# The beginning of a two-block transformer kernel: order of the modulation columns, and who multiplies them

## The chip, the cores and the metric

The kernel runs on one core of a Trainium2 chip. The metric is the device time of one execution in microseconds (us). Of three runs of the kernel before, the median is 2067.61 us.

## The reference

Two transformer blocks in turn on x (256 rows, 1024 columns, float32). The first has two layers with modulation. What the change touches is how layer 0 begins:

```
c_act = silu(c)                                  # 1024 values
mod = c_act @ ada_w[layer] + ada_b[layer]        # 1024 x 6144, gives 6 x 1024 values
sh1, sc1, g1, sh2, sc2, g2 = split(mod, 6)
h = rms_norm(x, norm_mix[layer]) * (1.0 + sc1) + sh1
x = x + g1 * mixer(h, ...)                       # begins with proj = h @ w_in[layer]
```

The mixer (three kinds of attention), a dense feed-forward part, a second layer with eight experts, and a second block (a state-space branch, windowed attention, a feed-forward part) follow. They are the same in both kernels.

## The kernel before, in words

All weights come as one stream, in slots of up to 1 MB, by DMAs that the SP queue issues in the order of the program. Layer 0 begins before the ring of slots is in use. Eight early slots (`EARLY_SLOTS`) hold the 2048 columns of `ada_w[0]` that make shift and scale. A unit `u` is 512 columns, slots 2u and 2u+1; slot 2u holds the row blocks k = 0 to 3, slot 2u+1 the row blocks 4 to 7. A slice is one k of a unit: 128 rows by 512 columns. Behind the early slots come the first ring slots (`load_to(3)`), which hold the first columns of `w_in`.

`mod` is wanted as columns: 128 values of it down the partitions, block by block. Two engines share a unit's eight slices.

- VectorE (`dve_mods`) takes the first `SUMS[u]` slices: each is multiplied by its value of `cact` per partition and added into `modsum` (128 x 512). The sum over the partitions is missing, and TensorE makes it in `pe_mods_sum`: four products of 128 columns of `modsum` with a column of ones.
- TensorE (`pe_mods`) takes the rest straight from the slot: four products for each slice, with one column (`cact`) as the moving side. Both add into the same PSUM bank, 2 or 3 by turns (`COLUMN`).
- `dve_mods_add` adds the bias and writes four columns of `K.mod`.

Once scale and shift of the first four blocks of 128 columns are there, `turned_part(0, 4)` forms these blocks of h, turned (they were transposed by `pe_turn` into PSUM), as a high and a low part (`hT`, `hTl`). `turned_part(4, 8)` forms the other four. Weights are split in a high part (ScalarE, `whi`) and a low part (VectorE, `wlo`) in parts (chunks) of a slot; `split_to(n)` brings the splits up to chunk n, and `BETWEEN` says at which blocks j of the forming the splits of the first stage `inA0` come in between. Every large product is three matmuls: high by high, high by low, low by high. `inA0` has four chunks of 12 matmuls of 416 columns.

Each engine runs a program written out in order by hand: `pe_start`, `dve_start`, `act_start`, then the mixer. An instruction waits for the semaphore counts of named events (`wait_ge`). In `pe_start` stand idle matmuls, `idle(n)`: n products of 128 x 128 by 256 columns of `colt` into bank 1, whose result nobody reads. The root of the row norms (`dve_eps`, `dve_root`) gives the factors that `pe_along` lays along the free dimension; `turned_part` waits for them.

Order before on TensorE: 10 idle, block of unit 0, 2 idle, closing sum 0, 1 idle, transposes of x, 3 idle, unit 1, 2 idle, sum 1, factors, 4 idle, unit 2, 2 idle, sum 2, 8 idle, unit 3, 2 idle, sum 3, 2 idle, projection.

Of the kernel before, what the change touches and what calls it, by code (L numbers as in the profile page):

```python
# [10 lines left out]
ALU = mybir.AluOpType  # L11
# [65 lines left out]
def ada(layer, c0, c1):  # L77
    return panels(f"ada{layer}", "ada_w", (layer,), KT, c0, c1)
# [7 lines left out]
def plan():  # L86
    p = []
    for l in range(2):
        into = [panels(f"inA{l}", "w_in", (l,), KT, 768, 1184), panels(f"inD{l}", "w_in", (l,), KT, 0, 512),
                panels(f"qup{l}", "w_q_up", (l,), 2, 0, 768) + panels(f"kvup{l}", "w_kv_up", (l,), 1, 0, 1024),  # L90
                panels(f"inB{l}", "w_in", (l,), KT, 1184, 1696),
                narrow(f"inV{l}", "w_in", (l,), 512, 768) + narrow(f"inV{l}", "w_in", (l,), 1696, 1952)]
        mod = summed(0, 2048) if l == 0 else []
        behind = {(1, 0), (1, 1), (2, 3), (3, 0)}
        for n, stage in enumerate(into):
            for at, slot in enumerate(stage):
                p.append(slot)
                if mod and (n, at) in behind:
                    p.append(mod.pop(0))
        if l == 0:  # L100
            p += summed(0, 3072) + summed(0, 4096)
        p += tapered(f"out{l}", "w_out", (l,))
        if l == 0:
            ffn = gate_up("ffn", "ffn_w_gate", "ffn_w_up", (0,)) + down("ffnd", "ffn_w_down", (0,))
            mod = summed(0, 5120) + [slot for c in range(0, 6144, 1024) for slot in summed(1, c)]
            for n, slot in enumerate(ffn):
                p += [slot] + (mod[n - 2:n - 1] if n > 1 else [])
        else:
            for e in range(NE):
                p += gate_up(f"moe{e}", "moe_w_gate", "moe_w_up", (0, e))  # L110
                p += down(f"moe{e}d", "moe_w_down", (0, e))
    w = "w_in_2"
    xbc = blocks_t("xbc", w, (0,), list(range(XBC0, XBC0 + 4096, 128)))
    p += xbc[:5] + panels("dt", w, (0,), KT, DT0, DT0 + 32) + xbc[5:]
    for c in (Q0, K0, V0):
        p += narrow("qkv0", w, (0,), c, c + 512)
    p += panels("z", w, (0,), KT, Z0, Z0 + 2048)
    p += panels("gs", w, (0,), KT, GS0, GS0 + 1024)
    p += panels("sproj", "w_ssd_proj_2", (0,), 16, 0, D)
    for g in (1, 2):  # L120
        for c in (Q0, K0, V0):
            p += narrow(f"qkv{g}", w, (0,), c + 512 * g, c + 512 * g + 512)
    p += narrow("ga", w, (0,), GA0, GA0 + 1024)
    p += panels("aproj", "w_attn_proj_2", (0,), 4, 0, D)
    p += tapered("out2", "w_out_2", (0,))
    p += blocks_t("up2", "w_up_2", (0,), [c for b in range(FT) for c in (128 * b, FF + 128 * b)])
    p += down("down2", "w_down_2", (0,))
    return p


def whole_plan():

    return ada(0, 0, 2048) + plan()


def offsets(p):
# [7 lines left out]


EARLY_SLOTS = 8

COLS = {}

# [79 lines left out]
class Tensor(Unit):  # L229
# [23 lines left out]
    def idle(self, b, n):  # L253

        self.take(b)
        for _ in range(n):
            self.mm(self.K.ps[b][:, 0:256], self.K.cst("ones"), self.K.cstt[:, 0:256], True, True)
# [369 lines left out]
def pe_start(K, pe):  # L627

    def idle(n):
        for _ in range(n):  # L630
            pe.mm(K.ps[1][:, 0:256], K.colt[:, 0:128], K.colt[:, 0:256], True, True)
    pe.wait_ge(K.s_cols, 32)
    idle(10)
    pe_mods(K, pe, 0)
    idle(2)
    pe_mods_sum(K, pe, 0)
    idle(1)
    pe.wait_ge(K.s_x, 16)
    pe_turn(K, pe, "nm0", lambda j, i: K.x[:, i, 128 * j:128 * j + 128], KT, "v")
    idle(3)  # L640
    pe_mods(K, pe, 1)
    idle(2)
    pe_mods_sum(K, pe, 1)
    pe_along(K, pe, "nm0")
    idle(4)
    pe_mods(K, pe, 2)
    idle(2)
    pe_mods_sum(K, pe, 2)
    idle(8)
    pe_mods(K, pe, 3)  # L650
    idle(2)
    pe_mods_sum(K, pe, 3)
    idle(2)

# [16 lines left out]
def dve_start(K, v):  # L671
    v.wait_ge(K.s_cols, 32)
    v.wait_ge(K.act, "rout_hi")
    v.tt(K.rout[:, 1, :], K.col("router", 0, 64), K.rout[:, 0, :].bitcast(F32), ALU.subtract, key="rout_lo")
    ang, n, r = K.ang, K.angn, K.angr
    v.copy(K.posf[:, :], K.posi[:, :])
    for i in range(2):
        v.ts(ang[:, i, :], K.col("invf", 0, 16), K.posf[:, i:i + 1], None, ALU.mult)
    for t, (shift, quarter) in enumerate(((0.0, 0.0), (0.25, float(np.float32(np.pi / 2))))):
        v.ts(n[:, :, :], ang[:, :, :], float(np.float32(1 / (2 * np.pi))), shift, ALU.mult, ALU.add)  # L680
        v.ts(n[:, :, :], n[:, :, :], MAGIC, None, ALU.add)
        v.ts(n[:, :, :], n[:, :, :], MAGIC, None, ALU.subtract)
        if t:
            v.wait_ge(K.act, ("turn", 0))
        v.stt(r[:, :, :], n[:, :, :], -TWO_PI_1, ang[:, :, :], ALU.mult, ALU.add)
        v.stt(r[:, :, :], n[:, :, :], -TWO_PI_2, r[:, :, :], ALU.mult, ALU.add)
        v.stt(r[:, :, :], n[:, :, :], -TWO_PI_3, r[:, :, :], ALU.mult, ALU.add)
        v.ts(r[:, :, :], r[:, :, :], quarter, 3.1415925, ALU.add, ALU.min)
        v.ts(r[:, :, :], r[:, :, :], -3.1415925, None, ALU.max, key=("angle", t))
    K.dve.here("angles")  # L690
    def turned_part(j0, j1):
        v.stt(K.sc[:, j0:j1], K.mod[:, 0, 8 + j0:8 + j1], 1.0, K.col("nm0", j0, j1 - j0), ALU.add, ALU.mult)
        v.last()
        dve_mod_t(K, v, "nm0", K.sc, shift_of(K, 0, 0), j0, j1)
    dve_mods(K, v, 0)
    dve_mods(K, v, 1)
    dve_mods_add(K, v, 0)
    dve_eps(K, v, "nm0")
    dve_root(K, v, "nm0")
    dve_mods(K, v, 2)  # L700
    dve_mods_add(K, v, 1)
    dve_mods_add(K, v, 2)
    turned_part(0, 4)
    dve_mods(K, v, 3)
    v.split_to(1)
    dve_mods_add(K, v, 3)
    turned_part(4, 8)

# [24 lines left out]
def dve_eps(K, v, s):  # L733
    v.wait_ge(K.act, (s, "sq", 0, 1))
    v.ts(K.ssq[:, 0:2], K.ssq[:, 0:2], EPS, None, ALU.add, key=(s, "eps"))


def dve_root(K, v, s):

    ms, t, rs = K.r_v[:, 0:2], K.r_t[:, 0:2], K.rs[:, 0:2]  # L740
    v.wait_ge(K.act, (s, "sq", 1, 1))
    v.tt(ms, K.ssq[:, 0:2], K.ssq[:, 2:4], ALU.add)
    v.wait_ge(K.act, (s, "sd"))
    v.recip(rs, K.sd[:, 0:2])
    v.stt(t, rs, -0.5, ms, ALU.mult, ALU.mult)
    v.tt(t, t, rs, ALU.mult)
    v.stt(rs, t, 1.5, rs, ALU.add, ALU.mult, key=(s, "rs"))
# [92 lines left out]
def dve_split_t(K, v, s, hi, lo, nblk):  # L840
    for j in range(nblk):
# [2 lines left out]

BETWEEN = {"nm0": ("inA0", {4: 2, 5: 3, 6: 4}), "nf0": ("ffng", {4: 3, 6: 4}), "nm1": ("inA1", {4: 3, 6: 4}), "n1": ("xbc", {4: 3, 6: 4}),
           "n2": ("up2", {4: 3, 6: 4})}


def split_between(K, x, s, j):

    stage, parts = BETWEEN.get(s, (None, {}))
    if j in parts:
# [18 lines left out]
def shift_of(K, layer, which):  # L873
    return K.mod[:, layer, 8 * which:8 * which + 8]
# [105 lines left out]


COLUMN = (2, 3)
SUMS = (6, 6, 6, 4)


def pe_mods(K, pe, u):
# [22 lines left out]
def dve_mods(K, v, u):  # L1009
    if u >= 2:  # L1010
        v.wait_ge(K.pe, ("modsum", u - 2))
    acc = K.modsum[:, u % 2, :]
    v.wait_ge(K.act, "cact")
    for k in range(SUMS[u]):
        n = 2 * u + k // 4
        v.wait_ge(K.s_early[n], 16)
        w, c = K.early[:, n, 512 * (k % 4):512 * (k % 4) + 512], K.cact[:, k:k + 1]
        if k == 0:
            v.ts(acc, w, c, None, ALU.mult)
        else:  # L1020
            v.stt(acc, w, c, acc, ALU.mult, ALU.add, key=("unit", u) if k == SUMS[u] - 1 else None)


def dve_mods_add(K, v, u):
    v.wait_ge(K.pe, ("modsum", u))
    v.tt(K.mod[:, 0, 4 * u:4 * u + 4], K.ps[COLUMN[u % 2]][:, 0:4], K.col("ab0", 4 * u, 4), ALU.add, key=("mods", u))


def pe_broadcast(K, pe, s, banks, halves=(0, 1)):
# [1870 lines left out]
def sync_program(K, sp):  # L2900
# [11 lines left out]
    load(K.s_x, (K.x[:, :, :], K.x_d.rearrange("(i p) d -> p i d", p=128)))  # L2912
    early(2, EARLY_SLOTS)
    sp.load_to(3)
# [21 lines left out]
class Kernel:  # L2936


    def __init__(self, nc, ctx, args):
# [7 lines left out]
        self.s_cols, self.s_first, self.s_rest, self.s_x = signal("columns"), signal("first_constants"), signal("other_inputs"), signal("rows_in")  # L2947
        self.s_early = [signal(f"modulation{n}") for n in range(EARLY_SLOTS)]
        self.s_bias, self.s_out, self.s_gates = signal("bias"), signal("stored"), signal("gate_biases")
# [3 lines left out]
        self.off, _ = offsets(whole_plan())  # L2953
        self.off = self.off[EARLY_SLOTS:]
        self.order_weights()
# [281 lines left out]
```

## Time and profile before

| | us |
|---|---|
| median of three runs | 2067.61 (2066.7 to 2067.73) |
| span of the profiled execution, first to last instruction | 2064.5 |
| TensorE matmul busy | 1977.9 (96%) |
| VectorE busy | 1661.1 (80%) |
| ScalarE busy | 1303.0 (63%) |
| mean granted TensorE clock | 0.985 of full speed |

The page gives no other time for the profiled execution than its span; the median lies 3.1 us above it. A matmul counts as busy also where it runs at half clock or moves a single column. Matmuls of plain float32 stand in the trace as two records each; those of the projection as one.

### The profile page before, as it was taken

What the parts mean: (1) busy time and instruction counts of PE and PEld (TensorE: products, weight loads), DVE (VectorE), ACT (ScalarE), POOL (GpSimd) and SP (SyncE); (2) the same over time, 40 slices, a digit from 0 to 9 for tenths busy, and PEclk for the clock granted to TensorE, in tenths of its full rate; (3) what the DMA queues carried; (4) which work ended last, traced back from release to release, by engine and by line L of the source; (5) the groups of instructions that cost most, each with busy time, mean ns of one, the idle gap of its engine ahead of it and who ended that gap; (6) DMA issues with size and microseconds to landing.
All of it is one profiled execution on the core that took longest, in us unless ns stands there. A gap on an engine that the chain in (4) does not pass through costs nothing. (4 is left out here: it accounts for less than half of the span.)

```text
span 2064.5 us, 28277 instructions
## 1 busy us (share of the span) xinstructions
PE 1977.9 (96%) x11261; PEld 1713.4 (83%) x11261; DVE 1661.1 (80%) x2113; ACT 1303.0 (63%) x1943; POOL 0.2 (0%) x4
## 2 busy tenths in 40 slices
PE   9879999988999999999999999989999999999999
PEld 8668788877778888888888888869988789989997
DVE  6876898677689989998999899978755667767884
ACT  3644534366678777787878787856565745536662
POOL 0000000000000000000000000000000000000000
PEclk9988999999999999999999999999999999999999
DMA  8625799741269989998999899955422444334553
GB/s 334 224 103 184 279 371 327 267 148 41 102 247 369 361 328 353 367 368 331 358 357 363 333 363 360 355 188 184 164 103 102 163 163 144 123 106 147 189 184 111
DMA packets 70810, 498.78 MB, mean 242 GB/s; under 512 B 8080, under 2 KB 8336, under 8 KB 11408
## 3 DMA queue, kind: packets, MB, share of 16 engines
q1 hardware_dynamic: 69952, 494.28, 64.7%
q10 hardware_dynamic: 720, 2.62, 0.3%
q8 instruction: 91, 1.49, 0.3%
q14 instruction: 47, 0.39, 0.0%
HBM read 495.82 MB, written 1.05 MB: 241 GB/s over the span
## 5 line engine op out<-in xcount | busy, mean ns | idle before, releaser
L352 DVE TENSOR_TENSOR wlo<-ring,whi 128x1024 fp32r<-128x1024 f32 (+1 forms) x845 | 1014.9, 1216 | 230.5 <-ACT whi L400 210.5
L400 ACT ACTIVATE whi<-ring 128x1024 fp32r<-128x1024 f32 (+1 forms) x845 | 884.1, 1054 | 469.5 <-PE ps L244 385.9
L244 PE MATMUL ps<-whi,hT 128*128 128x256 f32 (+2 forms) x944 | 315.1, 334 | 9.1 <-DVE wlo L352 3.9
L244 PE MATMUL ps<-whi,hTl 128*128 128x256 f32 (+2 forms) x944 | 309.4, 328 | 0.0
L244 PE MATMUL ps<-wlo,hT 128*128 128x256 f32 (+2 forms) x944 | 309.4, 328 | 0.0
L244 PE MATMUL ps<-whi,xg 128*128 128x512 f32 (+1 forms) x768 | 289.4, 377 | 1.3 <-DVE wlo L352 1.1
L244 PE MATMUL ps<-whi,xgl 128*128 128x512 f32 (+1 forms) x768 | 285.8, 372 | 0.0
L244 PE MATMUL ps<-wlo,xg 128*128 128x512 f32 (+1 forms) x768 | 285.5, 372 | 0.0
L244 PE MATMUL ps<-whi,hf 128*128 128x512 f32 x528 | 208.3, 395 | 4.8 <-DVE wlo L352 3.0
L244 PEld LDWEIGHTS ps<-whi,hT 128*128 128x128 f32 x944 | 180.4, 191 | 31.8 <-DVE wlo L352 7.7
L244 PE MATMUL ps<-wlo,hf 128*128 128x512 f32 x528 | 205.7, 390 | 0.0
L244 PEld LDWEIGHTS ps<-wlo,hT 128*128 128x128 f32 x944 | 180.5, 191 | 14.6 <-issue 0.5
L244 PEld LDWEIGHTS ps<-whi,hTl 128*128 128x128 f32 x944 | 180.2, 191 | 14.9
L244 PE MATMUL ps<-hT,whi 128*128 128x256 f32 (+1 forms) x616 | 175.1, 284 | 4.7 <-ACT hT L380 4.4
L244 PE MATMUL ps<-hTl,whi 128*128 128x256 f32 (+1 forms) x616 | 174.2, 283 | 0.0
L244 PE MATMUL ps<-hT,wlo 128*128 128x256 f32 (+1 forms) x616 | 174.2, 283 | 0.0
L244 PEld LDWEIGHTS ps<-whi,xg 128*128 128x128 f32 x768 | 144.7, 188 | 26.7 <-DVE wlo L352 1.9
L244 PEld LDWEIGHTS ps<-whi,xgl 128*128 128x128 f32 x768 | 144.6, 188 | 25.6
L244 PEld LDWEIGHTS ps<-wlo,xg 128*128 128x128 f32 x768 | 144.8, 189 | 24.4
L244 PE MATMUL ps<-whi,hf1l 128*128 128x512 f32 x352 | 137.3, 390 | 0.0
L244 PEld LDWEIGHTS ps<-hT,whi 128*128 128x128 f32 (+1 forms) x616 | 117.5, 191 | 5.9 <-ACT hT L380 5.1
L244 PEld LDWEIGHTS ps<-whi,hf 128*128 128x128 f32 x528 | 99.2, 188 | 26.0 <-DVE wlo L352 4.7
(298 smaller groups left out, 2625.0 us busy)
## 6 DMA issues: line engine op xcount, KB each, us to landing
ring<-in_wstream SPq DMA_DIRECT2D x454, 1024.0 KB, 5.3
work<-in_wstream SPq DMA_DIRECT2D x8, 1024.0 KB, 14.5
ring<-in_wstream SPq DMA_DIRECT2D x4, 832.0 KB, 14.5
modrow<-in_gates ACTq DMA_DIRECT2D x3, 512.0 KB, 6.9
ring<-in_wstream SPq DMA_DIRECT2D x6, 256.0 KB, 2.6
cst<-in_cst SPq DMA_DIRECT2D x1, 1028.0 KB, 26.0
x<-in_x SPq DMA_DIRECT2D x1, 1024.0 KB, 10.3
work<-in_bias ACTq DMA_DIRECT2D x2, 512.0 KB, 4.8
```

Source lines behind the costliest of these rows:

```text
L244: i = self.e.matmul(out, lhsT, rhs, start=start, stop=stop, skip_group_check=True)
L352: i = self.e.tensor_tensor(K.wlo[:, q % NS, 0:cols], src, hi.bitcast(F32), ALU.subtract)
L400: i = self.e.activation(K.whi[:, q % NS, 0:cols], K.ring[:, m % RING, at:at + cols], ACT.Copy)
```

## The change

The 2048 early columns of `ada_w[0]` are loaded in another order: scale columns 0 to 511 (from 1024 on), shift 0 to 511, scale 512 to 1023, shift 512 to 1023. Before they came as shift, shift, scale, scale. `dve_mods_add` writes and reads its columns by that order. Every unit is now halved: four slices for VectorE, four for TensorE. In `pe_start` the idle matmuls between block and closing sum are gone, and of the others some. In `dve_start` the root is taken between units 0 and 1 and the sum of unit 0, the first four blocks follow unit 2 with the sums of units 0 and 1, the sum of unit 2 comes after unit 3, and two chunks instead of one are split ahead of the last sum. `BETWEEN` has its second and third split one block later.

```diff
 def whole_plan():
-    return ada(0, 0, 2048) + plan()
+    return [slot for c in EARLY_COLUMNS for slot in ada(0, c, c + 512)] + plan()

+EARLY_COLUMNS = (1024, 0, 1536, 512)

 def pe_start(K, pe):
...
     pe.wait_ge(K.s_cols, 32)
-    idle(10)
+    idle(8)
     pe_mods(K, pe, 0)
-    idle(2)
     pe_mods_sum(K, pe, 0)
     idle(1)
     pe.wait_ge(K.s_x, 16)
     pe_turn(K, pe, "nm0", lambda j, i: K.x[:, i, 128 * j:128 * j + 128], KT, "v")
-    idle(3)
+    idle(2)
     pe_mods(K, pe, 1)
-    idle(2)
     pe_mods_sum(K, pe, 1)
     pe_along(K, pe, "nm0")
-    idle(4)
     pe_mods(K, pe, 2)
-    idle(2)
     pe_mods_sum(K, pe, 2)
-    idle(8)
+    idle(3)
     pe_mods(K, pe, 3)
-    idle(2)
     pe_mods_sum(K, pe, 3)
     idle(2)

 def dve_start(K, v):
...
     dve_mods(K, v, 0)
+    dve_eps(K, v, "nm0")
     dve_mods(K, v, 1)
+    dve_root(K, v, "nm0")
     dve_mods_add(K, v, 0)
-    dve_eps(K, v, "nm0")
-    dve_root(K, v, "nm0")
     dve_mods(K, v, 2)
     dve_mods_add(K, v, 1)
-    dve_mods_add(K, v, 2)
     turned_part(0, 4)
     dve_mods(K, v, 3)
-    v.split_to(1)
+    dve_mods_add(K, v, 2)
+    v.split_to(2)
     dve_mods_add(K, v, 3)
     turned_part(4, 8)

-BETWEEN = {"nm0": ("inA0", {4: 2, 5: 3, 6: 4}), ...
+BETWEEN = {"nm0": ("inA0", {4: 2, 6: 3, 7: 4}), ...

-SUMS = (6, 6, 6, 4)
+SUMS = (4, 4, 4, 4)

 def dve_mods_add(K, v, u):
     v.wait_ge(K.pe, ("modsum", u))
-    v.tt(K.mod[:, 0, 4 * u:4 * u + 4], K.ps[COLUMN[u % 2]][:, 0:4], K.col("ab0", 4 * u, 4), ALU.add, key=("mods", u))
+    c = EARLY_COLUMNS[u] // 128
+    v.tt(K.mod[:, 0, c:c + 4], K.ps[COLUMN[u % 2]][:, 0:4], K.col("ab0", c, 4), ALU.add, key=("mods", u))
```

## Rows read from the trace of the kernel before

**Rows 1.** The page's chain of waits, shares of the span by engine.

```profile
PE 29%; DVE 2%; ACT 2%; issue 0%; DVEq 0%; ACTq 0%
```

**Rows 2.** Timeline of TensorE, 0 to 60: start us, us, engine, line, what, count.

```profile
3.88 7.56 PE L244 MATMUL ps<-cols 128*128 128x256 f32 x20 [3.88 <-DMA posi<-in_pos]
...
15.26 1.91 PE L263 MATMUL ps<-cst,x 128*128 128x128 f32 x16
17.00 1.46 PE L244 MATMUL ps<-cols 128*128 128x256 f32 x6
18.37 1.95 PE L244 MATMUL ps<-cact,work 128*128 128x1 f32 x16
...
23.55 3.58 PE L244 MATMUL ps<-cols 128*128 128x256 f32 x8
26.92 1.89 PE L244 MATMUL ps<-cact,work 128*128 128x1 f32 x16
...
30.43 5.38 PE L244 MATMUL ps<-cols 128*128 128x256 f32 x16
35.65 3.63 PE L244 MATMUL ps<-cact,work 128*128 128x1 f32 x32
39.14 1.11 PE L244 MATMUL ps<-cols 128*128 128x256 f32 x4
40.08 1.17 PE L244 MATMUL ps<-cst,gate 128*128 128x1 f32 x8
41.11 2.05 PE L244 MATMUL ps<-cols 128*128 128x256 f32 x4
42.60 0.91 PE L244 MATMUL ps<-whi,hT 128*128 128x416 f32 x1
```

**Rows 3.** DMA issues on SP: last early slot, then issue to landing of three.

```profile
6.92 0.86 SPq L2904 DMA_DIRECT2D work<-in_wstream  x1
DMA to landing us min/median/max: 21.3/21.3/21.3
...
DMA to landing us min/median/max: 6.4/7.5/8.5
...
DMA to landing us min/median/max: 22.5/22.5/22.5
```

**Rows 4.** Timeline of VectorE, same columns; brackets: idle before and its releaser.

```profile
23.58 3.97 DVE L306 SCALAR_TENSOR_TENSOR gate<-work,cact,gate 128x512 f32<-128x512 f32 x5
...
41.29 0.16 DVE L299 TENSOR_TENSOR mod<-ps,cols 128x4 f32<-128x4 f32 x1 [2.60 <-PE ps L244]
...
42.08 1.01 DVE L352 TENSOR_TENSOR wlo<-ring,whi 128x832 fp32r<-128x832 f32 x1
...
47.52 0.48 DVE L306 SCALAR_TENSOR_TENSOR hTl<-aux,mod,hT 128x256 fp32r<-128x256 f32 x1 [0.19 <-ACT hT L382]
...
52.73 0.59 DVE L320 COPY work<-ps 128x416 f32<-128x416 f32 x1 [1.27 <-PE ps L244]
...
65.72 0.69 DVE L352 TENSOR_TENSOR wlo<-ring,whi 128x512 fp32r<-128x512 f32 x1 [0.39 <-ACT whi L400]
```

**Rows 5.** Busy time by stretch: length, PE, PEld, DVE, ACT, POOL, clock, DMA, GB/s.

```profile
23.40:26.80 3.40, 3.40 (x11) 2.78 (x11) 3.15 (x6) 0.38 (x1) 0.00 (x0) 0.53 1.01 422
26.80:30.20 3.40, 3.40 (x27) 3.21 (x27) 0.91 (x2) 0.00 (x0) 0.00 (x0) 0.97 1.00 412
30.20:33.65 3.45, 3.45 (x12) 2.82 (x12) 2.79 (x8) 1.41 (x3) 0.00 (x0) 0.53 1.03 424
37.06:40.50 3.44, 3.44 (x29) 3.34 (x29) 1.63 (x2) 0.00 (x0) 0.00 (x0) 1.00 0.65 236
40.50:43.90 3.40, 3.40 (x12) 3.01 (x12) 2.54 (x7) 1.67 (x3) 0.00 (x0) 0.52 0.02 5
```

**Rows 6.** Timeline of TensorE, 130 to 175, in the mixer, granted clock 0.51 there.

```profile
153.58 3.52 PE L244 MATMUL ps<-cst,work 128*128 128x1 f32 x16
156.96 1.95 PE L263 MATMUL ps<-cst,att_w 128*128 128x128 f32 x8
```

More of the change, by code:

```diff
@@ L843, in dve_split_t @@
         v.tt(lo[:, j, :], turned(K, j), hi[:, j, :].bitcast(F32), ALU.subtract, key=(s, "lo", j), own=False)
-BETWEEN = {"nm0": ("inA0", {4: 2, 5: 3, 6: 4}), "nf0": ("ffng", {4: 3, 6: 4}), "nm1": ("inA1", {4: 3, 6: 4}), "n1": ("xbc", {4: 3, 6: 4}),
+BETWEEN = {"nm0": ("inA0", {4: 2, 6: 3, 7: 4}), "nf0": ("ffng", {4: 3, 6: 4}), "nm1": ("inA1", {4: 3, 6: 4}), "n1": ("xbc", {4: 3, 6: 4}),
            "n2": ("up2", {4: 3, 6: 4})}
```

## The prediction

> **What bounds the kernel now.** The chain of waits comes first. Its shares add up to a third of the span [rows 1], so it covers only the last part of the program and says nothing on the beginning, where the whole change lies. I therefore read the beginning from the engines' own timelines.
>
> TensorE's timeline [rows 2] shows an engine with hardly a gap, but up to 42.60 it does no large product. It runs idle matmuls (`ps<-cols`), blocks of one-column products (`ps<-cact,work`), closing sums (`ps<-cst,gate`) and transposes. The first product of the input projection starts at 42.60. What released it is the engine's own order: closing sum of the last unit at 40.08, two idle matmuls at 41.11, product at 42.60. The last slot of modulation columns is issued at 6.92 and lands 21.3 later, at 28.2 [rows 3]. So the start is 14.4 us behind its data.
>
> VectorE's timeline [rows 4] tells who waits for whom later. VectorE waits 2.60 for the last closing sum (41.29), forms the second four blocks until 48.0, waits again for TensorE at 52.73 (the end of the projection's first stage), and then has no idle time that the view marks until 65.72. So a shift of TensorE at 42.60 moves its end of that stage, and with it VectorE's next work; ring slots are issued as splits free them and move too. I find no later resource with a date of its own, so I carry a shift of the start to the end of the kernel one for one.
>
> Third view: the granted clock by stretch [rows 5]. It is 0.53 (1.2 GHz) in 23.40:26.80, 30.20:33.65 and 40.50:43.90, and 2.4 GHz between. TensorE counts as busy in all of them. What differs is what it did before: 26.80:30.20 and 37.06:40.50 hold 27 and 29 records, mostly one-column, and both are followed by half clock. The stretch from 30.43, filled with eight idle matmuls of 256 columns, is followed by full clock at 35.65 [rows 2, 5]. A second sight of it is at 153.58 [rows 6]: sixteen one-column records in a row.
>
> **The prices.** The trace has two records for a matmul of this type; a column slice of the vector-matrix product is 4 matmuls, 8 records.
> - One-column record: 35.65 to 39.14 for 32, 0.109 us at full clock [rows 2]; 153.58 to 156.96 for 16, 0.211 at half clock [rows 6]. A block of four slices costs 3.5 or 6.8, a closing sum (8 records) 0.9 or 1.7.
> - Idle matmul: 17.00 to 18.37 for three, 0.46 at full; 23.55 to 26.92 for four, 0.84 at half [rows 2].
> - The 16 transposes: 15.26 to 17.00, 1.7 at full [rows 2]; at half 3.4, from eight in 1.95 [rows 6].
> - A slice on VectorE: 3.97 for five, 0.79 [rows 4].
>
> **The change part by part.**
> VectorE loses two slices in each of three units, 6 x 0.79 = 4.8 us. TensorE gets them: 48 more records. At full clock this is 5.2 us, at half 10.1. It also loses 2 + 2 + 2 + 2 idle matmuls between blocks and sums, 2 at the head, 1 before unit 1, 4 before unit 2 and 5 of the 8 before unit 3: 20 in all, 9.1 us at full clock and 16.8 at half. Counted alone this is a gain on TensorE.
>
> The new column order costs nothing: same slots, same bytes, same queue. It lets the first four blocks be formed after two units. These take VectorE some 3.8 us (the second four took 6.7, 41.29 to 48.0, with three splits of 1.0 in them [rows 4]), and with TensorE ahead they would be hidden; they are off TensorE's path since the first product comes after the last sum. The earlier root (before the sum of unit 0) makes the row factors ready before TensorE asks for them; before, it had to wait. Splitting two parts instead of one before the last sum takes one 1.0 us split out of the second four blocks; slot 4 of the ring is asked for earlier on SP's queue, behind nothing that waits.
>
> Now the walk of TensorE. Head: ten idle matmuls took 7.6 from 3.88; the last ones were at full clock, so two fewer end near 10.5, and the second slot lands at 10.6 (second of two issues from 1.64, 8.5 to landing [rows 3]). So it starts at 10.6.
>
> If the clock stays full: block 14.1, sum 15.0, idle 15.5, transposes 17.2, two idle 18.1; the fourth slot is there at 18.3; block 21.8, sum 22.7, factors along the rows (four small products, 0.109 each) 23.2, block 26.7, sum 27.6, three idle 29.0, block 32.5, sum 33.4, two idle 34.3. VectorE is not later than this: its unit 3 ends near 31, and its two splits near 33.3, since ring slot 0 lands at 7.82 + 22.5 = 30.3 [rows 3]. Start 34.3 against 42.60: 8.3 us won.
>
> But the clock will not stay full. In this walk TensorE does, from 18.3 to 27.6, nothing but one-column products and sums, with four small products between; from 10.6 to 15.0 too. Each stretch of that kind in the rows, shorter than these, had half clock behind it. I take half clock from 13.4 on, full clock once more behind the transposes, from 20.2 to 23.6, and half from there; the moments are my choice, as soon after the work as in rows 5. Three idle matmuls are little beside the eight from 30.43, and the two that stood between a block and a sum before did not keep the clock. Walk: 26 records until 13.4, six more at half, 14.7; sum 16.4; idle 17.2; transposes 20.6; two idle 21.5; 19 records until 23.6 and 13 at half, 26.3; sum 28.0; factors 28.8; block 35.6; sum 37.3; three idle 39.8; block 46.6; sum 48.3; two idle 50.0. The product starts at 50.0 against 42.60, 7.4 us late.
>
> VectorE hides in this case: first four blocks from 29.3 to 33.2, unit 3 by 36.1, two splits, then it waits 12 us for the last sum; the second four blocks end near 54 (6.7 less the split that has gone), ahead of TensorE's need at its third part (50.0 + 5). The 4.8 us that it saved buy nothing.
>
> The first part of the projection ran its first matmuls at half clock before too (42.60 to 43.90), so I add nothing for them. Both ends for what I can't see, the moments at which the clock moves. If the block at 39.8 is at full clock, 3.3 + 0.8 + 0.8 come off. If the projection's first 24 matmuls stay at half, they cost about 0.35 each instead of 0.19, 3.8 more, less about 0.5 that was paid before.
>
> The Trainium skill speaks against this walk in two places. "TensorE: Matmul & The Clock Gate", part 1 on the clock gate, says that the gate is set by how busy the engine has been lately. TensorE is 3.40 busy of 3.40 in 26.80:30.20, and half clock follows, so busy in the profile's sense is not enough; by that rule read plainly the start would be the 34.3 of the full clock. The same page, in its section on LDWEIGHTS, gives the load of the stationary operand as its columns over 1.2 GHz, whatever the gate does. A one-column product is all load, and here its record went from 0.109 to 0.211 with the clock, so the trace disagrees.
>
> **The rivals.**
> A, full clock throughout: the order of work above with no half-clock stretch, start 34.3, 8.3 less. For it: TensorE's busy share is complete, and 18.37's block of 16 records was not followed at once by half clock. Against it: all of rows 5. Time 2059.3. This is the other side; it decides where no one-column block is followed by 1.2 GHz.
> B, the clock returns before the last block, in the three idle matmuls: 50.0 less 4.9, start 45.1, 2.5 late, 2070.1. For it: stretches may fall so that the idle ones fill one.
> C, the half clock lasts into the projection: 7.4 + 3.3 = 10.7 late, 2078.3. For it: only two idle matmuls stand before it.
> D, one-column records cost 0.109 at either clock, only idle matmuls and transposes pay: 10.6, 14.1, 15.0, 15.9, 19.3, 20.2, 23.7, 24.6, 25.4, 28.9, 29.8, 32.3, 35.8, 36.7, 38.4; 4.2 less, 2063.4. Rows 6 speak against it. (The skill's section on LDWEIGHTS would give this.)
>
> **How the numbers follow.** The profiled execution has a span of 2064.5; the runs' median 2067.61 lies 3.1 above it, and I add the shift to the median: 2067.6 + 7.4 = 2075.0. Chances: forecast 0.60 (2072 to 2077.5 as its own range), C 0.12, B 0.14, A 0.10, D 0.04. What this kernel's measurement can tell from no change is 0.2%, 4.1 us: below 2063.5 faster, above 2071.7 slower. Slower: forecast and C, 0.72. Same: B and the upper half of D, 0.16. Faster: A and the rest, 0.12. The range 2067 to 2079 holds forecast, B and nearly all of C; A and D stay out.
>
> **What would show it.** Right: granted clock near 0.5 over most of 24 to 48; the last two blocks of 32 one-column records at 6.8 us each; first product near 50; VectorE waiting over 10 us for the last sum; its wait before the first four blocks; the same shift still there when it copies the first projected columns (52.73 before, about 60 after). Wrong: a last block of 3.5 us, or a first product before 43. If the start is late and the end is not, the carrying one for one has failed.

## The result, and the profile after

The changed kernel takes 2076.81 us (median of 20 runs, 2068.29 to 2080.30); the kernel before, run beside it, 2068.25 (20 runs, 2062.93 to 2079.10). The ratio is 1.0032, 95% interval [1.0021, 1.0042]: 8.6 us slower by the medians. Forecast: 2075.0, slower. The profiled execution took 2078.85, with a span of 2077.0 against 2064.5.

TensorE's timeline of the changed kernel in the beginning (start us, us, engine, line, what, count; in brackets the idle time before and what ended it) answers to [rows 2]:

```profile
3.80 6.64 PE L245 MATMUL ps<-cols 128*128 128x256 f32 x16 [3.80 <-DMA posi<-in_pos]
11.71 5.64 PE L245 MATMUL ps<-cact,work 128*128 128x1 f32 x32 [1.27 <-DMA work<-in_wstream]
17.22 1.85 PE L245 MATMUL ps<-cst,gate 128*128 128x1 f32 x8
18.92 1.20 PE L245 MATMUL ps<-cols 128*128 128x256 f32 x2
19.92 3.62 PE L264 MATMUL ps<-cst,x 128*128 128x128 f32 x16
23.33 1.07 PE L245 MATMUL ps<-cols 128*128 128x256 f32 x4
24.24 4.47 PE L245 MATMUL ps<-cact,work 128*128 128x1 f32 x32
28.56 1.84 PE L245 MATMUL ps<-cst,gate 128*128 128x1 f32 x8
30.27 1.20 PE L245 MATMUL ps<-cst,rs 128*128 128x128 f32 x4
31.26 6.83 PE L245 MATMUL ps<-cact,work 128*128 128x1 f32 x32
37.95 1.84 PE L245 MATMUL ps<-cst,gate 128*128 128x1 f32 x8
39.66 2.91 PE L245 MATMUL ps<-cols 128*128 128x256 f32 x6
42.36 6.83 PE L245 MATMUL ps<-cact,work 128*128 128x1 f32 x32
49.04 1.84 PE L245 MATMUL ps<-cst,gate 128*128 128x1 f32 x8
50.75 2.05 PE L245 MATMUL ps<-cols 128*128 128x256 f32 x4
52.24 0.91 PE L245 MATMUL ps<-whi,hT 128*128 128x416 f32 x1
```

The same 32 records that took 3.5 us at 35.65 before take 6.7 from start to start (31.26 to 37.95, 42.36 to 49.04), 0.209 us a record. The projection's first product comes at 52.24 instead of 42.60. The clock by stretch (length, busy time of the five engines, granted clock, DMA share, GB/s) answers to [rows 5]:

```profile
13.20:16.60 3.40, 3.40 (x18) 3.40 (x18) 0.17 (x1) 2.12 (x5) 0.00 (x0) 0.50 1.02 430
16.60:20.00 3.40, 3.40 (x15) 3.11 (x16) 2.90 (x5) 2.51 (x8) 0.00 (x0) 0.50 1.00 424
20.00:23.40 3.40, 3.40 (x18) 3.40 (x17) 2.29 (x8) 0.00 (x0) 0.00 (x0) 0.50 1.02 429
23.40:26.80 3.40, 3.40 (x29) 3.30 (x28) 1.27 (x2) 0.00 (x0) 0.00 (x0) 1.00 1.02 417
26.80:54.10 27.30, 27.30 (x117) 26.34 (x117) 11.44 (x25) 6.14 (x12) 0.00 (x0) 0.50 0.52 211
```

The clock is 1.2 GHz from about 13.2, has one spell of 2.4 GHz behind the transposes, and is then 1.2 GHz for 27.3 us without a break. TensorE counts as busy in all of it; only the clock column tells the fast spell from the slow ones. Weight loads (the second figure) are busy too, 26.34 of 27.30.

VectorE, answering to [rows 4], waits 9.06 for the last closing sum, where it waited 2.60, and copies the first projected columns at 62.56 instead of 52.73:

```profile
30.45 0.16 DVE L300 TENSOR_TENSOR mod<-ps,cols 128x4 f32<-128x4 f32 x1 [5.74 <-PE ps L245]
...
50.93 0.16 DVE L300 TENSOR_TENSOR mod<-ps,cols 128x4 f32<-128x4 f32 x1 [9.06 <-PE ps L245]
...
62.56 0.59 DVE L321 COPY work<-ps 128x416 f32<-128x416 f32 x1 [2.19 <-PE ps L245]
```

To follow the shift through the program I take ScalarE's table loads, rare and in the same order in both kernels. First the kernel before, then the changed one:

```profile
202.71 1.28 ACT L382 ACT_TABLE_LOAD   x1
...
1364.95 1.28 ACT L382 ACT_TABLE_LOAD   x1
...
1864.12 1.28 ACT L382 ACT_TABLE_LOAD   x1
```

```profile
212.73 1.28 ACT L383 ACT_TABLE_LOAD   x1
...
1374.74 1.28 ACT L383 ACT_TABLE_LOAD   x1
...
1876.64 1.28 ACT L383 ACT_TABLE_LOAD   x1
```

The shift is 10.0 at 203, 9.8 at 1365 and 12.5 at 1864. The start's 9.6 is carried whole; 2.7 us more come in the second block, in this pair of executions.

### The profile page after: what moved, and what is told of

Read it like the earlier page. It is cut to its first block and busy times, and to the rows that moved or that the text cites. A ratio compares the mean times of both kernels' runs of the same rounds, so it can differ in the third digit from the quotient of the medians.

```text
span 2077.0 us, 28285 instructions
## 1 busy us (share of the span) xinstructions
PE 1990.8 (96%) x11269; PEld 1727.2 (83%) x11269; DVE 1657.5 (80%) x2107; ACT 1303.4 (63%) x1943; POOL 0.2 (0%) x4
## 5 line engine op out<-in xcount | busy, mean ns | idle before, releaser
L245 PEld LDWEIGHTS ps<-whi,xgl 128*128 128x128 f32 x768 | 144.6, 188 | 25.6
```

Source lines behind the costliest of these rows:

```text
L245: i = self.e.matmul(out, lhsT, rhs, start=start, stop=stop, skip_group_check=True)
```

## The experiments

The theory: TensorE's clock drops behind one-column products, and the new beginning has long runs of them. Rival 1: the moved slices cost TensorE their records at any clock. Rival 2: the new orders (columns, VectorE) make the loss. Rival 3: the idle matmuls that were taken out had kept the clock. Rival 4: the late start is partly swallowed and something else makes the loss. In the table, "128-fold" means that each one-column product moves its column 128 times; the ratio is to the kernel before, run in the same batch.

| kernel | first product in its profile | median, us | ratio to before [95%] |
|---|---|---|---|
| changed | 52.24 | 2076.81 | 1.0032 [1.0021, 1.0042] |
| changed, 128-fold moving side | 34.97 | 2062.73 | 0.9968 [0.9956, 0.9981] |
| changed, 128-fold, again | 35.54 | 2061.11 | 0.9964 [0.9950, 0.9978] |
| before, 128-fold | 38.89 | 2063.26 | 0.9970 [0.9955, 0.9984] |
| before, 128-fold, again | 39.07 | 2064.36 | 0.9976 [0.9961, 0.9991] |
| changed, 32-fold | 48.96 | 2074.65 | 1.0022 [1.0007, 1.0037] |
| changed, idle matmuls back | 63.10 | 2089.77 | 1.0092 [1.0073, 1.0112] |
| changed, old shares | 41.81 | 2067.09 | 0.9984 [0.9972, 0.9996] |
| orders alone | 42.68 | 2068.04 | 0.9988 [0.9969, 1.0008] |
| before, 16 idle matmuls late | 50.41 | 2075.18 | 1.0029 [1.0010, 1.0047] |
| changed, 128-fold, old shares | 36.47 | 2060.64 | 0.9953 [0.9936, 0.9970] |
| changed, 128-fold, fewer idle | 33.33 | 2061.26 | 0.9953 [0.9938, 0.9969] |
| as the last, other sums 64-fold | 33.55 | 2061.27 | 0.9958 [0.9942, 0.9975] |

**The same products with 128 columns in place of one.** The products and their loads stay; what moves is the same column 128 times, and one result of the 128 is read.

```diff
-            pe.mm(K.ps[b][:, j:j + 1], K.early[...], K.cact[:, k:k + 1], ...)
+            pe.mm(K.ps[b][:, 128 * j:128 * j + 128], K.early[...], K.cact[:, k:k + 1].to_broadcast([128, 128]), ...)
-        pe.mm(K.ps[b][:, j:j + 1], K.modsum[...], K.cst("ones")[:, 0:1], False, True,
+        pe.mm(K.ps[b][:, 128 * j:128 * j + 128], K.modsum[...], K.cst("ones")[:, 0:128], False, True,
-    ... K.ps[COLUMN[u % 2]][:, 0:4] ...
+    ... K.ps[COLUMN[u % 2]].rearrange("p (j n) -> p j n", j=4)[:, :, 0] ...
```

> The changed kernel, but each one-column product of the modulation (blocks and closing sums) moves the same column 128 times: the moving side is broadcast to 128 columns, one of which is read. Same loads of the stationary side, same number of matmuls, same order. Theory (the half clock behind one-column work makes the loss): clock 2.4 GHz through the beginning from about 10 on, a block of 32 records 3.5 us each time, first product of the projection at 34 to 35, time about 2068.3 - 8 = 2060 (0.996 of the kernel before). Rival 1 (the slices moved to TensorE cost it their records at any clock): the blocks stay near 6 us, first product near 50, 2077. Rival 2 (VectorE's new order or the new column order makes the loss): first product near 50 and VectorE idle in another place, 2077.

TensorE's timeline of this kernel, and below it its clock in one stretch:

```profile
28.53 1.46 PE L245 MATMUL ps<-cols 128*128 128x256 f32 x6
29.83 3.73 PE L245 MATMUL ps<-cact,work 128*128 128x128 f32 x32
33.40 1.05 PE L245 MATMUL ps<-cst,gate 128*128 128x128 f32 x8
34.30 1.03 PE L245 MATMUL ps<-cols 128*128 128x256 f32 x4
34.97 0.54 PE L245 MATMUL ps<-whi,hT 128*128 128x416 f32 x1
```

```profile
10.00:39.00 29.00, 27.83 (x217) 26.96 (x218) 21.28 (x46) 11.91 (x25) 0.00 (x0) 1.00 1.00 412
```

With 128 times the moving columns a record takes 0.112 us (29.83 to 33.40 for 32) instead of 0.209, against 0.109 for one column at full clock. The streaming of the columns adds next to nothing; that it hides behind the load is my reading. The clock is full from 10 to 39, the start comes 17.3 us earlier than in the changed kernel, and the time is 2062.7 instead of 2076.8 (another batch; 6.3 below its own kernel before instead of 8.6 above). That is 2.7 above the 2060 expected. Rivals 1 and 2 are out as the cause of the loss: moved slices and orders are all still there, and the loss is not.

> The kernel before with the same 128-fold moving side. Theory: its three half-clock stretches before 44 go, first product at 38 to 39 instead of 42.6, time about 2064 (0.998). Compared with the changed kernel in the same form it tells what the rest of the change is worth when the clock is out of play: 4 us by the theory (38.3 against 34.1). Rival 1 (moved slices cost what they cost) expects this one to be the faster of the two.

The kernel before gains from it as well: the start is 38.89, and it gains more than expected in time (5.8 us by the medians). The 4 us expected between the two kernels in this form did not show: 2063.26 against 2062.73, though the starts lie 3.9 apart. They were run once more for this, below. The profiled execution gains only 0.2 in span (2064.3 against 2064.5), although it starts 3.7 earlier; single executions compare poorly at the end, as told under the carry.

**A quarter of the columns.** As the first, with 32 for 128.

> The changed kernel with the moving side 32-fold, a quarter of the streaming. Theory: not enough beside the loads everywhere, so the clock still falls in part; start between those of one column (52.2) and 128 columns (35.0), 42 to 50, time 2068 to 2074. If any more than one column is enough: 35, 2062.

The start is 48.96, nearly as late as the theory allows; the time is a little above what was expected. TensorE's timeline shows the block of the third unit from 27.98 to 34.67, 6.7 us, the price at half clock:

```profile
27.98 6.87 PE L245 MATMUL ps<-cact,work 128*128 128x32 f32 x32
34.67 1.90 PE L245 MATMUL ps<-cst,gate 128*128 128x32 f32 x8
...
39.08 6.87 PE L245 MATMUL ps<-cact,work 128*128 128x32 f32 x32
```

With 32 columns the clock falls much as with one: it is 0.50 from 26.8 to 50.6, as it is from 26.8 to 54.1 in the changed kernel.

**The idle matmuls back.** `pe_start` of the kernel before (10, 2, 1, 3, 2, 4, 2, 8, 2, 2 idle matmuls) in the changed kernel.

> The changed kernel with the idle matmuls of the kernel before (10, 2, 1, 3, 2, 4, 2, 8, 2, 2). Theory (it is the long runs of one-column work that drop the clock, whichever idle matmuls stand between): blocks still at 5 to 6.8 us, the 20 idle matmuls come on top, first product at 51 to 60, time 2080 to 2086, slower than the changed kernel. Rival 3 (the idle matmuls taken out are what kept the clock): clock as before, first product near 45 (42.6 plus the 48 records at full clock less what hides), time 2069 to 2071.

The start is 63.10 and the time 2089.8. Both lie beyond the theory's figures (60 and 2086), and on the side opposite to rival 3. Its timeline, third and fourth unit:

```profile
37.63 6.83 PE L245 MATMUL ps<-cact,work 128*128 128x1 f32 x32
...
47.73 6.00 PE L245 MATMUL ps<-cols 128*128 128x256 f32 x16
53.57 4.76 PE L245 MATMUL ps<-cact,work 128*128 128x1 f32 x32
```

The eight idle matmuls take 5.8 us (47.73 to 53.57), themselves at half clock for the most part, to win 2.1 of the 6.7 us of the block behind them (53.57 to 58.19 in that timeline). Rival 3 is out; with halved units, taking idle matmuls out is the part of the change that helps.

**The old shares.**

```diff
-SUMS = (4, 4, 4, 4)
+SUMS = (6, 6, 6, 4)
```

> The changed kernel with the old shares (6, 6, 6, 4): VectorE takes six slices of the first three units, TensorE two; fewer idle matmuls, new column order and new order on VectorE stay. Theory: one-column blocks are short again, first product near 42, time 2066 to 2068, no slower than the kernel before. Rival 3 (missing idle matmuls) and rival 2 (orders) both expect it to stay near 2077, first product near 50.

As the theory had it, undoing the halving alone gives the whole loss back, and a little more (start 41.81, ratio 0.9984). The clock is mostly half here too (0.51 over 23.40:44.00), but there are 48 fewer records to pay for, 10.0 us at 0.209 each, and the removed idle matmuls pay. So the loss is the product of both: more one-column records, and half clock under them. The stretch, and the blocks of units 2 and 3:

```profile
23.40:44.00 20.60, 20.60 (x85) 19.63 (x86) 15.07 (x30) 6.47 (x12) 0.00 (x0) 0.51 0.91 365
```

```profile
24.25 3.41 PE L245 MATMUL ps<-cact,work 128*128 128x1 f32 x16
...
31.93 6.83 PE L245 MATMUL ps<-cact,work 128*128 128x1 f32 x32
```

**Orders alone.** Old shares and old idle matmuls; column order, VectorE's order and the second early split stay.

> The changed kernel with the old shares (6, 6, 6, 4) and the old idle matmuls: left are the column order, the earlier root, the first four blocks formed between units 2 and 3, and the second early split. Theory: TensorE's work is that of the kernel before and so is its clock; factors on TensorE are ready earlier by about 1 us, so start 41 to 42.6, time 2067 to 2069 (0.999 to 1.000). Rival 2 (the orders make the loss) expects it above 2073.

The start is 42.68 against 42.60, and the ratio is 0.9988 with 1 inside its interval. The orders neither harm nor help in a way that can be told.

**A pure delay.** The kernel before with 18 idle matmuls behind the last closing sum instead of 2.

```diff
     pe_mods_sum(K, pe, 3)
-    idle(2)
+    idle(18)
```

> The kernel before with 16 more idle matmuls after the last closing sum (18 instead of 2): a pure delay of the projection on TensorE, 16 x 0.46 = 7.3 us at full clock. VectorE and the DMAs go on. Theory (a shift of the projection's start is carried to the end one for one): start near 50, time 2069 + 7.3 = 2076, as the changed kernel. Rival 4 (later stages have slack that swallows part of a late start, and the changed kernel's loss has another part): clearly below 2076, 2071 to 2073.

```profile
38.94 1.71 PE L244 MATMUL ps<-cst,gate 128*128 128x1 f32 x8
40.51 10.26 PE L244 MATMUL ps<-cols 128*128 128x256 f32 x36
50.41 0.54 PE L244 MATMUL ps<-whi,hT 128*128 128x416 f32 x1
```

The start comes at 50.41, 7.8 later than in the kernel before, the span is 7.9 longer (2072.4 against 2064.5), and the median is 5.7 above that of the kernel before in the same batch (2069.51). The interval of the ratio allows 2.1 to 9.7 us, so this run alone does not exclude that some of a late start is swallowed. All runs together speak against rival 4. From the idle matmuls put back (start 20.5 later, median 20.7 up) to the leanest kernel below (9.3 earlier, 8.3 down), the median moves by the start's shift, to within 2.2 us in each of the thirteen rows of the table.

**Toward a better kernel.** The 128-fold form without the three idle matmuls before the last unit and the two before the projection:

> The changed kernel with the 128-fold moving side, and without the three idle matmuls before the last unit and the two before the projection. Theory: the clock stays full because the products themselves move columns; start 32.6 to 33.5 (last slot lands at 28 to 28.8, block 3.6, sum 0.9) against 35.0 with them, 1.5 to 2.4 us less than that kernel, time near 2061 (0.996). If the idle matmuls held the clock after all, a half-clock stretch shows near 30 to 37 and the start is no earlier than 35.

The clock stays full (1.00 from 10 to 39) and the start is 33.33, but the time is hardly below the form with them. The start's 1.64 us are gone further down: TensorE's transposes that wait for VectorE come at 56.88 here and at 57.17 there. ScalarE's timeline of this kernel shows why:

```profile
37.97 0.51 ACT L383 ACTIVATE hT<-aux,mod 128x256 fp32r<-128x256 f32 x1 [0.30 <-DVE aux L307]
39.52 0.38 ACTq L1440 DMA_DIRECT2D work<-in_bias  x1
39.93 0.45 ACTq L625 DMA_DIRECT2D modrow<-in_gates  x1
40.48 2.01 ACT L401 ACTIVATE whi<-ring 128x1024 fp32r<-128x1024 f32 x2 [1.99 <-PE ps L245]
42.67 0.52 ACT L381 ACTIVATE work<-ps 128x416 f32<-128x416 f32 x1 [0.18 <-PE ps L245]
44.73 1.06 ACT L401 ACTIVATE whi<-ring 128x1024 fp32r<-128x1024 f32 x1 [1.54 <-DMA ring<-in_wstream]
```

It has nothing to do from 38.5 to 39.5. Its program waits there for the last constants; their DMA is issued at 13.4 and lands 26.1 later, at 39.5. At 44.73 it has waited 1.54 us for a ring slot. In the form with the idle matmuls the same work comes 0.1 us later, without a wait for the DMA, so of the earlier start hardly anything is left here:

```profile
44.84 1.05 ACT L401 ACTIVATE whi<-ring 128x1024 fp32r<-128x1024 f32 x1
```

With a start below about 35, DMAs set the pace here.

> As wide_lean, and the one-column closing sums of the other modulation columns, in the mixer of layer 0 and later, move 64 columns each instead of one (PSUM has room for 64). Theory: the two such sums in the half-clock stretches near 150 to 170 take 3.4 us each there; if TensorE is what the stage waits for, 1 to 3 us less than wide_lean (near 2059); if VectorE is (12.3 busy of 13.6 us there), no difference.

No difference (2061.27 against 2061.26). VectorE is busy 25.6 of the 30 us from 135 to 165, and TensorE 21.7, so VectorE probably limits that stage; that is argued, not shown.

> The changed kernel with 128-fold moving side and the old shares (6, 6, 6, 4). With the clock out of play this is the price of the halving alone: TensorE has 16 records less in three units (1.75 us each at full clock), VectorE 1.6 us more in each. Both wait for slots landing 5 us apart, so start within 1 us of wide_after (35.0) and the time within 1 us of it.

With the clock out of play the halving of the units brings nothing: 2060.64 with old shares, 2062.73 and 2061.11 with halves (the latter in the same batch). The start is 0.9 to 1.5 us later (36.47), and the end no later.

> The changed kernel with 128-fold moving side once more, next to the other one on the same chip, because their starts (35.0 and 38.9) and their medians (2062.7 and 2063.3) do not agree. If the start is carried one for one: 3.9 us below the other. If the kernels end alike although one starts earlier, something between swallows it in most executions: 0 to 1 us below.

> The kernel before with 128-fold moving side once more. Carried one for one: about 2064 where the other has 2060. Otherwise both near 2063. The trace is to show whether its loss of 3 us at about 1370 (found in its first profile) comes again.

This time the changed order is 3.2 us ahead of the old one, where the first pair had 0.5; the starts differ by 3.5 to 3.9. So most of the earlier start may well reach the end, and the loss near 1370 did come again in the old order. It is smaller than the 3 us expected: between its table loads at 1362.92 and 1386.05 pass 23.1 us, 21.6 in the other:

```profile
1362.92 1.28 ACT L382 ACT_TABLE_LOAD   x1
...
1386.05 1.28 ACT L382 ACT_TABLE_LOAD   x1
```

```profile
1357.91 1.28 ACT L383 ACT_TABLE_LOAD   x1
...
1379.54 1.28 ACT L383 ACT_TABLE_LOAD   x1
```

The granted clock is 0.83 in both halves of the first one's 1355:1375 and 1.00 in the second one's 1350:1370. The loss does not belong to the old order. The first 128-fold form of the changed kernel has it too (1356.38 to 1379.41, 23.0 us, clock 0.83 in 1360:1370), and the kernel before does not (1364.95 to 1386.57, 21.6). Why the clock falls there in one execution and not in another stays open.

## Why the prediction was right

**The bound.** That the start of the projection is set by TensorE's own order, and that what sets TensorE's order in time is the clock, held. The price of a one-column record at half clock, read as 0.211 us, came out as 0.209 in the changed kernel; the closing sum at 1.71 (1.7), three idle matmuls at 2.70 (2.5).

**The walk.** The start was put at 50.0 and came at 52.24. The miss is all in the first block. TensorE waits 1.27 us for the second slot and begins at 11.71, where I had 10.6 from the kernel before; the clock falls at 13.2 all the same, so fewer of the 32 records are at full clock, and the block takes 5.5 us (11.71 to 17.22) instead of 4.1. That is 2.5 us; all later steps together take 0.3 less than in the walk. The spell of full clock came at 23.4 and not at 20.2, about as much later as the end of the transposes (23.3 and not 20.6). The moments at which the clock moves had been chosen, not derived, and that they fit this well is in part luck. The pure delay above runs the program of the kernel before up to 38.94, and in it the clock moves at other moments: the eight idle matmuls before the last unit take 3.5 us where they took 5.2, and the last block 4.6 where it took 3.5.

**VectorE.** The first four blocks begin at 31.99 (29.3 in the walk), as late as TensorE is: unit 1's sum is done near 30.3 instead of 28.0, VectorE waits 5.74 for it and 1.19 more for the row factors. It waits 9.06 for the last sum, where the sign named was over 10 and the walk said 12. The 12 comes out only without the two splits ahead of that wait; by the walk's own figures, 36.1 and two splits of 1.0 against 48.3, it is 10.2. That VectorE gives up 4.8 us of work and gains nothing by it was right.

**The carry.** One for one held for a late start: 9.6 at the start, 10.0 at 203, 9.8 at 1365, and a pure delay of 7.8 comes out as 7.9 in the profiled pair (5.7 by the medians). Behind that the profiled executions part by several us of their own: with the idle matmuls back the shift is 20.5 at the start, 21.8 at the table load that stands at 202.71 before, and 27.9 at the end, where the medians have 20.7. So the medians are the better witness for the end. The step's reason, that there is "no later resource with a date of its own", is wrong for an early start: at 33.33 the DMAs' dates are next. Had rival A come true (start 34.3), some of its 8.3 us might not have arrived: the 128-fold form, which is rival A in fact, starts 7.1 to 7.6 earlier than the kernel before and is 6.3 and 6.7 us faster by the medians of its batches (2069.06 and 2067.81 for the kernel before).

**The size.** 7.4 us were forecast and 8.6 measured; the median of 2076.81 lies inside the likeliest case's own range (2072 to 2077.5). Single runs of the changed kernel go from 2068.29 to 2080.30. The profiled pair has 12.5, and the 2.7 us that come late in it were not foreseen.

**The Trainium skill's two places.** "TensorE: Matmul & The Clock Gate", Part 1 (The HAM clock gate), has the gate go by how busy the engine has been. The profile's busy figure is full in all the stretches at 1.2 GHz above; the 128-fold form, with the same loads and a busy share that is no higher (27.83 of 29.00 us), stays at 2.4 GHz. The measurement decides: the busy share of the profile does not tell which clock is granted here. The same page's rule for a load, in its section "LDWEIGHTS (loading the stationary operand)", has no term for the clock and would leave a record at either clock alike; it takes 0.109 us at full clock and 0.209 at half.

## What to carry to other kernels

A matrix-vector product with the matrix as the stationary side is nearly all load: weight loads are busy 26.34 of 27.30 us here. TensorE looks busy, and yet behind a run of such products the clock fell to half, and a record took 0.209 us instead of 0.109. Before giving TensorE such work, read the granted clock of a stretch that has it, and price the work at that clock. In this kernel, broadcasting the moving side to 128 columns cost almost nothing (0.112 against 0.109 us a record) and kept the clock, where idle matmuls cost 0.46 to 0.84 us each.

## What the runs showed that I had not expected

- The kernel before spreads widely from run to run: 2061.98 to 2079.19 (35 runs), 2063.11 to 2077.57 (27), 2063.84 to 2082.09 (33). Its 128-fold form, in the last two of these batches, has 2060.95 to 2067.07 and 2060.92 to 2067.26 (12 runs each). The spread goes with the clock: in the last batch the run of 2063.84 has a mean granted clock of 0.985 and the run of 2082.09 has 0.978, while the 128-fold form beside it stays within 0.984 to 0.988. I take it that most of the spread is in how the clock falls in the first 45 us; no trace of an execution near 2079 was taken, so that is not shown.
- By the medians the 128-fold form gives the kernel before 5.8 and 3.5 us; the start in the profiled executions is 3.7 and 3.5 earlier. Each of the other runs on record takes 1.7 to 1.9 us more than its span, so the profiled execution of the kernel before took about 2066.3, which is 1.3 to 3.2 below the medians on record. It is a fast one of its kind, and differences of spans to it make the other kernels look slower at the end than the medians do.
- The fastest kernels here by ratio (2060.64 and 2061.26, 0.9953 each) owe this to the moving side and, as far as the runs can tell, to fewer idle matmuls, not to the halving: the first of them has the old shares.
